# Three seven-product pairs in a row, with their weight sums made in the first feed forward and kept in DRAM

## The reference

```python
# first block
x_new = x_new + g2 * sq_relu_mlp(hx2, w_mlp1[i], w_mlp2[i])      # square(relu(h @ w1)) @ w2
# second block
h = rmsnorm(x, norm_ffn[layer])
x = x + (jax.nn.silu(h @ w_gate[layer]) * (h @ w_up[layer])) @ w_down[layer]
...
D_FF_2 = ((8 * D_MODEL + 767) // 768) * 256          # 2816, eleven chunks of 256
```

## Time and profile before

| | |
|---|---|
| median of 3 runs | 721.08 us (720.75 to 721.64) |
| profiled execution | 720.66 us, its span 718.9 us |
| TensorE busy | 709.1 us (99%) |
| VectorE busy | 555.8 us (77%) |
| ScalarE busy | 424.6 us (59%) |
| GpSimd busy | 25.9 us (4%) |
| DMA | 152.22 MB, 212 GB/s in the mean |

### The profile page before, as it was taken

The page is one execution under the profiler, slowest core; times in us unless marked ns, Lnnn a source line. Parts: engine busy times, 40 slices in busy tenths (PEclk is TensorE's granted clock), DMA queues, the critical chain, the costliest instruction groups (busy, mean ns, idle before and its releaser), DMA issues.

```text
span 718.9 us, 9667 instructions
## 1 busy us (share of the span) xinstructions
PE 709.1 (99%) x3722; PEld 567.9 (79%) x3722; DVE 555.8 (77%) x949; ACT 424.6 (59%) x701; POOL 25.9 (4%) x43
## 2 busy tenths in 40 slices
PE   8999999999999999999999999999999999999996
PEld 4678885588888888888888777778888888888885
DVE  4789999898666757756998799855857988678933
ACT  4487658995754654546645677666456466436712
POOL 1030012001000000000010000000000000000000
PEclk9999999999999999999999999999999999999999
DMA  9996939617556585744548433344375598568501
GB/s 366 415 378 224 387 104 357 218 59 263 197 179 231 214 289 196 268 146 154 163 144 300 172 118 118 119 172 178 118 233 175 197 313 310 181 230 316 209 1 58
DMA packets 71932, 152.22 MB, mean 212 GB/s; under 512 B 4096, under 2 KB 19456, under 8 KB 70864
## 3 DMA queue, kind: packets, MB, share of 16 engines
q1 hardware_dynamic: 70080, 146.32, 57.4%
q0 software_dynamic: 1520, 5.03, 2.0%
q10 hardware_dynamic: 288, 0.27, 0.1%
HBM read 150.56 MB, written 1.05 MB: 211 GB/s over the span
## 4 chain that ended last, share of the span: by engine, by line
PE 91%; ACT 3%; issue 2%; DMA 2%; DVE 1%; POOL 0%; POOLq 0%; DVEq 0%; SPq 0%
PE bank L511 23%; PE bank L513 23%; PE bank L512 23%; PE bank L856 5%; PE bank L493 5%; PE bank L854 3%; DMA W<-in_w_in 2%; ACT WH L1185 1%; PE bank L530 1%; PE bank L988 1%; PE bank L1010 1%; PE bank L694 1%; PE bank L716 1%; PE bank L570 1%; PE bank L853 1%
## 5 line engine op out<-in xcount | busy, mean ns | idle before, releaser
L1720 DVE TENSOR_TENSOR WL<-W,WH 128x1024 fp32r<-128x1024 f32 (+2 forms) x234 | 263.4, 1173 | 27.0 <-ACT WH L1185 26.7
L1185 ACT ACTIVATE WH<-W 128x1024 fp32r<-128x1024 f32 (+2 forms) x234 | 222.9, 1013 | 55.7 <-DMA W<-in_w_mlp 35.8
L511 PE MATMUL bank<-WH,AHL 128*128 128x512 f32 (+1 forms) x440 | 173.1, 393 | 0.0
L513 PE MATMUL bank<-WH,AHL 128*128 128x512 f32 (+1 forms) x440 | 169.7, 386 | 0.0
L512 PE MATMUL bank<-WL,AHL 128*128 128x512 f32 (+1 forms) x440 | 169.6, 385 | 0.0
L511 PEld LDWEIGHTS bank<-WH,AHL 128*128 128x128 f32 x440 | 82.7, 188 | 19.0 <-issue 3.2
L513 PEld LDWEIGHTS bank<-WH,AHL 128*128 128x128 f32 x440 | 82.6, 188 | 16.9
L512 PEld LDWEIGHTS bank<-WL,AHL 128*128 128x128 f32 x440 | 82.8, 188 | 15.4
L511 PE MATMUL bank<-WH,HH 128*128 128x512 f32 (+1 forms) x218 | 84.9, 390 | 0.0
L513 PE MATMUL bank<-WH,HL 128*128 128x512 f32 (+1 forms) x218 | 84.5, 388 | 0.0
L512 PE MATMUL bank<-WL,HH 128*128 128x512 f32 (+1 forms) x218 | 84.4, 387 | 0.0
(11 more groups left out here) (307 smaller groups left out, 937.8 us busy)
## 6 DMA issues: line engine op xcount, KB each, us to landing
W<-in_w_mlp SPq DMA_DIRECT2D x32, 1024.0 KB, 5.4
W<-in_w_in SPq DMA_DIRECT2D x24, 1024.0 KB, 5.1
W<-in_w_down SPq DMA_DIRECT2D x11, 1024.0 KB, 5.1
W<-in_w_ada SPq DMA_DIRECT2D x10, 1024.0 KB, 8.0
WX<-in_w_ada SPq DMA_DIRECT2D x10, 1024.0 KB, 10.0
W<-in_w_out SPq DMA_DIRECT2D x8, 1024.0 KB, 5.2
W<-in_w_up SPq DMA_DIRECT2D x8, 1024.0 KB, 5.1
W<-in_w_gate SPq DMA_DIRECT2D x14, 512.0 KB, 4.0
```

Of the source, the lines that this page charges most:

```text
L511: e.matmul(po, hs, wh[:, k, c0:c0 + cw], start=first and k == 0, stop=False, skip_group_check=onto)
L513: ins = e.matmul(po, ls, wh[:, k, c0:c0 + cw], start=False, stop=last and k == unit.nk - 1, skip_group_check=onto)
L1185: e.activation(m.WH[unit.slot][:, c], m.W32[unit.slot][:, c], ACT.Copy).then_inc(S["w_hi"], 1)
L1720: e.tensor_tensor(m.WL[unit.slot][:, c], m.W32[unit.slot][:, c], m.WH[unit.slot][:, c].bitcast(F32), ALU.subtract).then_inc(S["w_lo"], 1)
```

## The change

`PAIRS` becomes (3, 5, 7): chunks 5 and 6 become a pair too, `NG` is 8, and three pairs follow each other. The sums of all three are no longer made in place by `make`: `STORED` names the three pairs, and `kept_sums` makes their sums in the first feed forward, in `STEPS` = 12 steps, four for each pair, one for each 128 rows of the half contraction. In a step GpSimd loads 128 rows of both halves of w_up and w_gate (two DMAs of 512 KB) into the tile `m.sums` (8 KB per partition, at the place of the second gate buffer), VectorE makes four sums of 128x512, and GpSimd stores the tile (1 MB) to a DRAM tensor `sums`. `SUMS_AT` says how many steps VectorE takes at each of 14 places of its program: one at all of them but places 6 and 8, the ones behind the low parts of rounds 4 and 5. In the second feed forward SyncE loads the four blocks of sums of a pair from `sums` instead of from the weights. `m.GW` is a single buffer. `small_out` waits for the last store, since `small` lies over the tile.

```diff
-PAIRS = (3,7)
+PAIRS = (3, 5, 7)
+STORED = (3, 5, 7)
+STEPS = 4 * len(STORED)
+SUMS_AT = (1, 1, 1, 1, 1, 1, 0, 1, 0, 1, 1, 1, 1, 1)
...
     def quad_unit(g, n, src, i):
...
+        if GROUPS[g][0] in STORED and n in (1, 2, 4, 6):
+            s = STORED.index(GROUPS[g][0])
+            kept = d["sums"][s, {4: 0, 2: 1, 1: 2, 6: 3}[n]].rearrange("p (k n) -> p k n", k=4)
+            units[-1].pieces = [(0, 512, kept)]
+            units[-1].kept = 48 * (4 * s + 4)
...
     def gate_rows(n):
         w.wait_ge(S["out_mm"], 8)
-        if n > 1:
-            w.wait_ge(S["g2"], 2 * n - 2)
+        if n:
+            w.wait_ge(S["g2"], 2 * n)
...
+        if unit.kept:
+            w.wait_ge(S["l_sums"], unit.kept)
...
     e.dma_start(m.g1b[:, :], d["final_g"].to_broadcast([128, D])).then_inc(S["l_gain"], 16)
+    w.wait_ge(S["out_mm"], 8)
+    for s in range(STEPS):
+        c0, kt = 256 * STORED[s // 4], s % 4
+        if s:
+            w.wait_ge(S["l_sums"], 48 * s)
+        for i, src in enumerate(("w_up_2", "w_gate_2")):
+            rows = d[src][:, c0:c0 + 512].rearrange("(h k p) n -> p k h n", h=2, p=128)[:, kt, :, :]
+            e.dma_start(m.sums[:, 2 * i:2 * i + 2, :], rows).then_inc(S["l_sums"], 16)
+        w.wait_ge(S["made"], 4 * s + 4)
+        kept = d["sums"][s // 4, :, :, 512 * kt:512 * kt + 512].rearrange("i p n -> p i n")
+        e.dma_start(kept, m.sums[:, :, :]).then_inc(S["l_sums"], 16)
     power(6)
...
+    if not GROUPS[NG - 2][1]:
+        up2(NG - 1, 0)
...
     def small_out(tb):
+        w.wait_ge(S["l_sums"], 48 * STEPS)
...
+    def kept_sums(place):
+
+        for s in range(sum(SUMS_AT[:place]), sum(SUMS_AT[:place + 1])):
+            u0, u1, g0, g1 = (m.sums[:, i, :] for i in range(4))
+            w.wait_ge(S["l_sums"], 48 * s + 32)
+            tt(g0, u0, g0, ALU.subtract, "made")
+            tt(u0, u1, u0, ALU.subtract, "made")
+            w.wait_ge(S["made"], 4 * s + 1)
+            tt(u1, u1, g0, ALU.subtract, "made")
+            w.wait_ge(S["made"], 4 * s + 3)
+            tt(g1, g1, u1, ALU.subtract, "made")
...
     hid_lo(0, 4, 1, 2)
     lo(2)
+    kept_sums(0)
     for tb in range(2):
         hid_lo(1, 4, tb, 3 + tb)
     lo()
+    kept_sums(1)
     for c in range(2, 7):
...
         low_wide(c, 0)
         low_wide(c, 1)
+        kept_sums(2 * c - 2)
         lo(2)
         if c < 6:
             gate_rows(2 * c - 4)
             gate_rows(2 * c - 3)
         else:
             gate_add()
+        kept_sums(2 * c - 1)
+    kept_sums(12)
     sum_wide(7, 0)
     sum_wide(7, 1)
     lo()
...
     low_wide(7, 0)
     low_wide(7, 1)
     lo()
+    kept_sums(13)
...
+    def in_place(g):
+        return GROUPS[g][1] and GROUPS[g][0] not in STORED
```

More of the change, by code:

```diff
@@ L107, in __init__ @@
         self.onesR = M("onesR", 84.8125, [128, 1], F32R)
-        self.GW = [M(f"GW{i}", 60 + 8 * i, [128, 2, D]) for i in range(2)]
+        self.GW = M("GW", 60, [128, 2, D])
+        self.sums = M("sums", 68, [128, 4, 512])
         self.gacc = M("gacc", 76, [128, D])
@@ L166 @@
 out_mm o1_hi o1_lo res1 nscale_dve nscale_act n_turned n_dve n_act kn
-l_g0 l_g1 g2 g2_hi g2_mm
+l_g0 l_sums g2 g2_hi g2_mm
 m1_mm m1_up m2_mm mlp_sum mlp_act hid_turned hid_hi hid_lo btw
@@ L196, in __init__ @@
         self.nk, self.wid, self.pieces, self.split, self.free = nk, wid, pieces, split, free
-        self.base = None
+        self.base, self.kept = None, 0
     def block(self, m):
@@ L314, in weight_units @@
             b11, t1, t2, b22, t3, b21, t4 = by["gu", g]
-            loads += [b11, t1, t2, *down, t4, b22, t3, b21]
+            if GROUPS[g][0] in STORED:
+                loads += [b11, t1, t2, *down, b22, t3, b21, t4]
+            else:
+                loads += [b11, t1, t2, *down, t4, b22, t3, b21]
             continue
@@ L359, in weight_units @@
         unit.lo = (S["w_lo"], 2 * u)
-    for n, g in enumerate(g for g in range(NG) if GROUPS[g][1]):
+    for n, g in enumerate(g for g in range(NG) if GROUPS[g][1] and GROUPS[g][0] not in STORED):
         t1, t2, _, t3, _, t4 = by["gu", g][1:]
@@ L363, in weight_units @@
             unit.base = unit.landed
-        t1.landed, t2.landed, t4.landed, t3.landed = ((S["made"], 8 * n + 2 * i + 2) for i in range(4))
+        t1.landed, t2.landed, t4.landed, t3.landed = ((S["made"], 4 * STEPS + 8 * n + 2 * i + 2) for i in range(4))
     return units, loads, by
@@ L374, in gate_rows @@
         w.wait_ge(S["out_mm"], 8)
[L375 to L376 removed]
+        if n:
+            w.wait_ge(S["g2"], 2 * n)
         src = d["w_ada"][256 * n:256 * n + 256, 5120:6144].rearrange("(k p) n -> p k n", p=128)
[L378 removed]
+        e.dma_start(m.GW[:, :, :], src).then_inc(S["l_g0"], 16)
     def load(n):
@@ L1091, in down2 @@
             for i, unit in enumerate(by["dn", g]):
-                part(unit, m.HH[g % 2], m.HL[g % 2], 2 * i, tb, 2 * n + tb, first and i == 0, last, "dn_mm",
+                part(unit, m.HH[g % 2], m.HL[g % 2], 2 * i, tb, 2 * n + tb, first and i == 0, last and i == GROUPS[g][1], "dn_mm",
                      lambda k: ("hid_lo", 16 + 2 * g + tb + 1), 512 * n, 512)
@@ L2137, in gate_rows @@
         n = k8 // 2
-        w.wait_ge(S[f"l_g{n % 2}"], 16 * (n // 2) + 16)
-        rows, ck = m.GW[n % 2][:, k8 % 2, :], m.cs[:, 2 * k8:2 * k8 + 1]
+        w.wait_ge(S["l_g0"], 16 * n + 16)
+        rows, ck = m.GW[:, k8 % 2, :], m.cs[:, 2 * k8:2 * k8 + 1]
         if k8:
@@ L2458, in quad_group @@
         q = quads.index(g)
-        following = GROUPS[g + 1][1]
-        make(g, 2)
+        made, following = in_place(g), in_place(g + 1)
+        if made:
+            make(g, 2)
         lo()
@@ L2466, in quad_group @@
         tt(m.u1, bank[5][:, :], m.g1[:, :], ALU.add, "quad")
-        make(g, 3)
+        if made:
+            make(g, 3)
         lo()
@@ L2513, in vector_program @@
         else:
-            following = GROUPS[g + 1][1]
+            following = in_place(g + 1)
             if following:
@@ L2573, in build_program @@
         S = {name: ctx.enter_context(nc.semaphore(name)) for name in NAMES}
+        d = dict(d, sums=nc.dram_tensor("sums", (len(STORED), 4, 128, 2048), F32, kind="Internal").ap())
         units, loads, by = weight_units(d, S)
```

1 line of the change is left out of this document (removed).

## The result

The changed kernel took 785.25 us in the median of 4 runs (783.81 to 786.90); the kernel before, on the same chip, 721.36. The ratio is 1.089, 95% interval 1.0858 to 1.0921. 761 us was forecast, with 739 to 795 as the range: the direction, the range and the mechanism of the main term hold, and the middle was 24 us short. The profiled execution took 783.8 us with a span of 782.0, 63.1 longer than before.

The account below looks back on a forecast made before the run. The prediction took a gapless TensorE stream as the bound. To the profiled 720.66 us it added 42.8 for late transposes, less 2.7 for 12 matmuls, +40.1: 760.8, or 761 us for the median, range 739 to 795.

Parts of the forecast that it names:

- What bounds the kernel: Whole kernel: a TensorE stream, busy for 99% of the span, that everything else just keeps fed.
- the 12 matmuls: Chunks 5 and 6 as a pair need 12 matmuls less, taking 2.7 us off the TensorE stream.
- The decisive term: First feed forward: with one buffer, VectorE waits in its queue for store then loads; transposes come 42.8 us late.
- R: Time from a step's last subtraction to the next tiles landed, one store and a pair of loads: 12 us.
- (b): Rival of crowded queues in the first feed forward: R about 15, 788 us; chance 0.24 for 775 to 810.
- rival (a): Short round trip in the first feed forward: R about 9, 740 us; chance 0.19 for 727 to 748.
- The walk: VectorE's order in the first feed forward, each step at the later of place and landing: transposes 42.8 us late.
- empty places: Two places without a step, before steps 6 and 7: these steps done at 300.7 and 321.7, nothing lost.
- The clock: TensorE's standing costs it clock: 0 in the sum, up to 4 us in the range.
- The second feed forward: In-place sums go without gain, weights may run late: 0, range 0 to 3 us; 2.7 us shorter by fewer matmuls.
- rival d: Second feed forward: the third pair itself starves for weights, 0 to 3 us on top; no chance given.
- step 10: Step directly behind step 9 in the first feed forward, nothing covering R: largest wait, about 12 us.

Follow-up runs that it names:

- pairs apart and the end moved: The run pairs apart, with the last group's second gate and up product moved ahead of the down products behind the last pair: 720.87 us, ratio 0.9994.
- run without transfers: The pairs alone plus the 48 subtractions on a tile filled once, with no loads or stores of sums: 729.94 us.
- two buffers: The changed kernel with the steps alternating between two tiles, each with its own semaphore: 746.95 us, ratio 1.0358.
- steps alone: The kernel before with its two pairs and in-place sums, plus the twelve steps, whose stored sums nobody reads: 777.16 us, ratio 1.0771.
- pairs alone: The changed kernel without steps, plain weight blocks loaded in place of the sums: 728.54 us, ratio 1.0099 against the kernel before.
- low part behind one split: The pairs alone, with VectorE making the first low part at a joint after one block's down splits instead of two: 721.60 us, ratio 1.0007.
- pairs apart: The changed kernel with pairs at groups 2, 5 and 8, the first one's sums stored in four steps, the others' made in place: 725.96 us.
- run with one pair stored: The changed kernel with only the middle pair's sums stored, in four steps at places 0, 3, 5 and 7, the others' in place: 734.54 us.
- run without subtractions: The pairs alone plus the twelve loads and stores chained on GpSimd, without subtractions or waits for them on VectorE: 748.25 us.

## Why the prediction was right, and where it was not

**What bounds the kernel, and the 12 matmuls.** Right. In the run with the pairs apart and the end moved, TensorE's stream ends 1.4 us earlier, which is the 2.7 us less the 1.2 that were lost on the way.

**The decisive term.** Right in kind: one buffer, VectorE waiting in its own queue, a store and a pair of loads one after the other. The run without transfers (+1.4 us), the one with two buffers (-38 us) and the one with the steps alone (+55.9) show it, each from another side. The term was mis-sized. R was taken as 12; it measured 10.6 where nothing else moved and 12 to 19 elsewhere, 14.2 in the mean. By the prediction's own cases that is (b), R over 13.5, to which it gave 0.24, and the time of 785 lies among that case's 775 to 810. The work on VectorE was put at 35 us and took 31. The prediction chose the ordinary landing of a weight load for each leg and added 0.5 for crowding and semaphores together; the gate rows' 7.1 us, which it held for the far end, was the nearer row in the loaded rounds. The fit in the Trainium skill (DMA: Bandwidth & Descriptors, "Anatomy of one DMA") gives an estimate of 4.4 us for 1 MB. The legs alone, 4.9 and 5.4 us between 380 and 391 us, lie 0.5 and 1.0 above it, and with the weight loads beside them the two took up to 18.6 us, so this case's trace decides against rival (a) and its R near 9.

**The walk.** Its rule held, and its last link, from the last step's end to the transposes, took 10.5 us for 10.7. The last step starts at 390.72 instead of the walk's 378.4, 12.3 us later; the transposes come 54.65 us late instead of 42.8, 11.8 later. In between it was too mild early: up_wide(4) begins at 265.68, 14.3 us late for 4.1, up_wide(5) at 298.32, 24.7 for 11.7, up_wide(7) at 354.74, 35.9 for 11.7. Between up_wide(5) and up_wide(7) it counted no new delay, for the empty places; 11.2 us came. The waits for a tile in these rounds are short (none at 310.74, then 0.85 and 0.94 us), so VectorE's own work was the limit there as much as the transfers, and how the 11.2 us divide no run shows. A step in one of the empty places changed nothing. In rival (a), 361.2 less 338.5 is 22.7 and not 21.8, which makes it 741 us; nothing hangs on that. And TensorE's loss was not one stand of 25 us before the last down blocks but eight waits of 0.8 to 11.3 us with slow matmuls behind them.

**The clock.** 0 in the sum fits the first feed forward: the slow stretches are there (0.79 granted from 360 to 400), but VectorE waited for no matmul between 200 and 393 us, the chain of steps set the end, and from the last step's end to the transposes passed 10.5 us (10.7 in the earlier trace rows). No run takes the lower clock away there. In the second feed forward nothing covered it, and there it counts.

**The second feed forward.** This is the step that failed. "Transposes and down products stay as many. ... I take 0 for this, 0 to 3 us for the range." The prediction counted products and bytes of three pairs in a row and looked for a ring that starves (rival d); the ring never starved (the loads from `sums` land after 5.5 us). What is late is VectorE's low part, since a pair behind a pair has no product that covers it. Two joints cost 3.6 us each against the ordinary distance (4.41 from the turns to the next matmul for 0.80) and some 1.5 each for the matmuls at the lower clock, 10.3 in all; less the 2.7 us of the 12 matmuls these are the 7.6 us up to the last matmul. The pairs alone (+7.3 us), the low part behind one split (back to 721.60) and the pairs apart show it. The order of products at the joint stands in the code and in no row of before, so the term was left at nothing without a look at it.

**The sum again, with what was measured:** 760.8 + 11.8 (R and the empty places) + 10.3 (two joints) + 0.6 (behind the last matmul) + 0.3 (between the feed forwards) = 783.8 us, the profiled execution's time. Rival (b), R about 15 with 788 us, was the nearest of the cases in the total, but partly by luck: it puts 69.5 us into the first feed forward, where 54.65 came, and nothing at the joints.

**The signs that were named.** Stores about 15 us apart where the steps stand close: 16.0, 14.6 and 13.2 for the last four; over all 13.2 to 21.2, 17.1 in the mean. Loads at 5 to 6 us to landing: 4.6 and 5.2 in the median between 200 and 400 us. Waits twelve, 60 us or more, largest 12 at step 10: ten, 56.0, 11.95 at step 10. The transposes about 43 us later: 54.65. TensorE standing 25 us before the last down blocks: 11.3. Second feed forward 2.7 us shorter: 8.2 longer, more than the 3 us at which the text called itself wrong.

## What to carry to other kernels

Where one engine waits in its own queue for a transfer whose buffer is freed only by the transfer before, count round trips and not bytes or busy shares: twelve of them, 17.1 us apart with their step, set the end here, while from 240 to 280 us VectorE was busy for 68% and the DMA engines for 74%. Place such steps more than a round trip apart (four of them, 22 us and more apart, cost 0.5 us) or give them a second buffer, and then check the bytes, which come next. When blocks of a new kind are put side by side, read the order at their joint: what covered the low part before may be missing, and one split moved behind it was worth 6.9 us in the pairs alone.

## What the runs showed that was not expected

- A wait of 3.4 us on TensorE can cost nearly twice its length. After 3.38 us the starts were 0.43 us apart for 15 matmuls in one trace, for 7 at the second joint of the same trace, and not at all in another (693.07 above), whose execution has the lowest time of its five (724.63, the others up to 728.10). In the run with one pair stored, waits of 2.15 and 1.95 us had stretches at 0.43 behind them too. After 1.11 us they stayed at 0.23 at both joints. What decides between them no run here shows.
- A 1 MB store issued by GpSimd landed after 4.6 us where nothing else moved, 6.3 in the median of the change, 10.3 with the DMA engines at 0.91 and 1.00 of their time in the stretches shown; weight loads went from 5.4 to 8.8 with it.
- An idle-looking engine's queue is a resource: with GpSimd issuing the chain (the run without subtractions), VectorE waited 9.2 us for a power of 0.5 us.
